# Transposes of the attention output and of the decayed keys: from TensorE to DMA, in a two-layer hybrid decoder step

## The chip, the cores and the metric

One Trainium2 chip, all 8 of its cores. Each core runs the same program on its own share: one prompt sequence of 2048 tokens (with 16 meta tokens ahead of it) and 16 of the 128 sample sequences of 4 tokens each. The cores don't talk to each other. The metric is the device time in microseconds of the slowest core.

## The reference

Two layers, each with two branches on the same normalised input, and gates that merge them:

```python
xn = rmsnorm(h, norm_g)
q, k, v, ga, u, gb, alow, mg = split(xn @ w_in)
la = log_sigmoid(alow @ w_alpha + b_alpha) / 16          # per token and key channel
# branch A, gated linear attention: 4 heads, keys 128 wide, values 256 wide
b = cumsum(la)                                           # within a chunk
o = (q exp(b)) (k exp(-b))^T, causal, @ v  +  (q exp(b)) @ S
S = exp(b_C) * S + (k exp(b_C - b))^T @ v                # b_C: b of the chunk's last token
o = o * rsqrt(mean(o*o) + EPS) * gla_gain * silu(ga)
ya = o @ w_a
# branch B: trailing means over 2/4/8/16 tokens minus the token, a small product, silu(gb), @ w_b
merged = sigmoid(mg_a + bias) * ya + sigmoid(mg_b + bias) * yb
h = h + merged @ w_out
```

Returned are the final outputs of prompt and samples and the new states of both branches. What the change touches is `o` after its norm, and `k exp(b_C - b)`, the decayed keys that go into the state S.

## The kernel before

**Tiling.** Activations lie transposed in on-chip memory (features on the 128 partitions, tokens along the row): XN is the normalised input, OT the finished output of branch A, YP that of branch B, MB decays and later the merged result. Tokens are cut into five chunks c = 0 to 4 of 464, 384, 384, 384 and 512 columns; chunk 0 holds the samples (64 columns), the 16 meta tokens and three prompt tiles of 128 tokens, the others 3, 3, 3 and 4 prompt tiles. Matrix products are bf16 with f32 sums.

**Stages.** Per layer: norm and transpose of the input (`stage_d`), decays (`alpha`), branch B (`pool_unit`), then attention as 4 heads times 5 chunks of `att_unit`, then for each of 8 column blocks and 5 chunks a `merge_unit`, which reads all heads' blocks of OT. Head 0 is woven with branch B, and heads 1 to 3 run with `sample_batch` (per head four of them, each with a load of 512 KB of sample states and a store of as much) and `sample_out` between the units.

**An attention unit** (`att_unit`, L902): keys are projected and scaled; GpSimd multiplies them by the decay at the tile's end into kdT (features on partitions); queries and values are projected (v_tok: tokens on partitions, two buffers that units take in turn); scores are computed and masked into ATm. kdT is needed with tokens on partitions. TensorE transposes it, one instruction for each 128x128 block, into a PSUM bank, and ScalarE copies the bank to kd_tok. Then two projections of the gate path go through tanh into the buffers zb. Then tiles are taken in pairs (one pair and one single tile where a chunk has three): `kd_tok x v` gives the state's increment (`bp`), two products give the output `o_`, VectorE updates the state (f32) and casts it to bf16 for the next tile, ScalarE squares and sums `o_`, GpSimd does the inverse root, and ScalarE writes the normalised output `on`. At the unit's end TensorE transposes `on`, two blocks for each tile, into a bank, and VectorE multiplies it with gain and gate into OT.

**What sets the order.** `Sched` records all operations; `list_schedule` then fixes one order for each engine beforehand, by assumed costs and by the order of recording. On the chip every engine, TensorE and the SyncE queue (SP) too, works in that fixed order and waits where an operand is not there. For its plan a DMA on SP is assumed to cost the queue 60 ns, to occupy a transfer resource shared by all DMAs for bytes / 200 ns, and to land 1.8 us later. Waits come from keys: a region of X or Y has one key for each 256 bytes of a row.

**Lines.** Products are recorded at L551, transposes at L556, scalar_tensor_tensor at L591, copies and casts at L598, tensor_tensor at L579, DMAs at L611; they are helpers, so a group of the trace is told by its tiles. All of kdT, kd_tok, on, ATm, v_tok, the states and zb lie in sb_X; sample states, their bf16 copy and kdm in sb_Y. `sb_ident_bf,sb_X` at L556 is thus a transpose of kdT or on, `sb_Y<-sb_ar,sb_invcnt` the build of kdm, the masked sample keys (kd0 in sb_ar times the masks in sb_invcnt).

Of the kernel before, what the change touches and what calls it, by code (L numbers as in the profile page):

```python
# [7 lines left out]
F32 = mybir.dt.float32  # L8
# [5 lines left out]
NL = 2  # L14
# [353 lines left out]
def build_nc():  # L368
# [30 lines left out]
    with contextlib.ExitStack() as st:  # L399
# [25 lines left out]
        X = Region("X", 25600)  # L425
# [10 lines left out]
        negc = sb("negc", [128, NCOLS], F32)  # L436
# [22 lines left out]
        kd_tok, kd_tok_k = X.take(512, BF16)  # L459
        ATm, ATm_k = X.take(512, BF16)  # L460
        on, on_k = X.take(1024, BF16)
        zb = [X.take(512) for _ in range(3)]
# [42 lines left out]

        def ot_rest(c):
            return ["ot%d_%d" % (c, h) for h in range(1, 4)] + (["ots_%d" % h for h in range(1, 4)] if c == 0 else [])


        mrg = []  # L510
        for i in range(2):
            a = X.take(512, at=2048 + i * 4096)
            b = X.take(512, at=2048 + i * 4096 + 2048)
            mrg.append((a, b))
        a = X.take(512, at=0)
        b = X.take(512, at=10240)
        mrg.append((a, b))
# [164 lines left out]
        def consts():  # L682
# [3 lines left out]
            ts("dve", negc[:, :], cols[:, :], -1.0, r=["cols"], w=["negc"])  # L686
# [95 lines left out]
        def alpha(l, c, wal):  # L782
# [9 lines left out]
            for h in range(4):  # L792
                bl, blk = bank("G")
                mm(bl[:, 0:N], wst[:, h * 128:(h + 1) * 128], ast[:, 0:N], True, True, r=["wst", "ast"],
                   w=[blk])
                act(b_ap(c, h), bl[:, 0:N], AF.Exp, r=[blk, "negc"], w=b_keys(c, h),
                    bias=negc[:, l * 40 + CL_BA + h:l * 40 + CL_BA + h + 1], scale=-1.0)
# [104 lines left out]
        def att_unit(l, h, c, wqk, wv, wga):  # L902
# [9 lines left out]
            v_ap, vk = v_tok[p]  # L912
            ek, bk = "ebc%d" % p, b_keys(c, h)
# [64 lines left out]
            bt, btk = bank("G")  # L978
            btb = bfv(bt)
            for j in range(nt):  # L980
                s_ = slice(base + j * 128, base + (j + 1) * 128)
                tr(btb[:, j * 128:(j + 1) * 128], kdT[:, s_], ident_bf[:, :], r=kdT_k + ["ident_bf"], w=[btk])
            if c == 0:
                tr(btb[0:NM, 512:640], kdT[:, 0:NM], ident_bf[:, :], r=kdT_k + ["ident_bf"], w=[btk])
                cp("act", kd0[0:NM, :], btb[0:NM, 512:640], r=[btk], w=kd0_k)
            cp("act", kd_tok[:, 0:nt * 128], btb[:, 0:nt * 128], r=[btk], w=kd_tok_k)
# [25 lines left out]
            for j0 in range(0, nt, 2):  # L1012
# [9 lines left out]
                for jj, j in enumerate(pr):  # L1022
# [325 lines left out]
```

How the kernel before makes its waits and increments, by code:

```python
            def run_engine(ename, eng):  # L294
                seen = {}
                for op in ops:
                    if op["eng"] != ename:
                        continue
                    need = {}
                    for d in op["kept"]:
                        sk, val = ops[d]["token"]
                        if need.get(sk, 0) < val:
                            need[sk] = val
                    items = [(sk, val) for sk, val in need.items() if seen.get(sk, 0) < val]
                    attach = items.pop() if (items and op.get("attach")) else None
                    for sk, val in items:
                        eng.wait_ge(sems[sk], val)
                        seen[sk] = val
                    inst = op["fn"](eng)
                    if attach is not None:
                        inst._wait_ge(sems[attach[0]], attach[1])
                        seen[attach[0]] = attach[1]
                    if op["token"] is not None:
                        sk, val = op["token"]
                        inst.then_inc(sems[sk], 16 if op["dma"] else 1)
                if ename == "sp":
                    for k, v in self.dma_final.items():
                        sk = ("dma",) + k
                        if seen.get(sk, 0) < v:
                            eng.wait_ge(sems[sk], v)
```

## Time and profile before

| | us |
|---|---|
| time, median of 3 runs (lowest to highest) | 1240.41 (1240.02 to 1241.66) |
| the profiled execution: its time | 1240.96 |
| its span on the slowest core (core 6) | 1239.1 |
| spans of the eight cores | 1231.7 to 1239.1 |
| granted clock, mean of each core | 0.982 to 0.988 |
| VectorE, ScalarE, GpSimd busy | 709.3, 554.7, 463.7 |
| queue of hardware DMAs (SP): MB, share of 16 engines' span | 81.46, 20.2% |
| queue of software DMAs (GpSimd): MB, share | 35.98, 18.8% |

A busy time adds up instructions from start to end; those of TensorE overlap a little, as their ends are modelled. "Idle before, releaser" is the time in which an engine stood before instructions of a group, and what ended it. A DMA's landing is the time from issue to completion.

### The profile page before, as it was taken

How to read it: one execution, taken by the hardware profiler on the slowest of the kernel's cores; microseconds unless marked ns; L12 is line 12 of the kernel's file. 1: busy time of each engine (PE TensorE's matmuls, PEld its weight loads, DVE VectorE, ACT ScalarE, POOL GpSimd, SP SyncE). 2: the span in 40 equal slices, each digit the busy share in tenths (PEclk: the TensorE clock that was granted, in tenths of full speed). 3: DMA queues.
4: the chain of work that ended last, by engine and by line, in shares of the span. 5: the costliest groups of instructions: out<-in, count | busy, mean ns of one | idle time of the engine just before them, and what ended most of it. 6: DMA issues, size and time to landing. Idle time of an engine off the chain costs nothing.

```text
span 1239.1 us, 22649 instructions; the slowest of 8 cores (1231.7 to 1239.1 us)
## 1 busy us (share of the span) xinstructions
PE 1159.9 (94%) x7554; PEld 694.3 (56%) x7616; DVE 709.3 (57%) x1278; ACT 554.7 (45%) x1255; POOL 463.7 (37%) x730
## 2 busy tenths in 40 slices
PE   2778889999999999999999899999999999999997
PEld 1434446677676555555545555676767655555543
DVE  6478867767675222237676876676777422223555
ACT  3555455665664222222653644656656422222222
POOL 3268655333333222221236666433342222222221
PEclk9789899999999999999999999999999999999999
DMA  9711037252429113114364513725242813211544
GB/s 238 150 52 39 18 67 174 77 137 77 112 69 189 31 30 64 19 29 154 133 165 135 103 38 84 145 66 131 69 103 86 190 30 58 37 18 26 179 160 156
DMA packets 68591, 118.90 MB, mean 96 GB/s; under 512 B 4188, under 2 KB 46556, under 8 KB 68442
## 3 DMA queue, kind: packets, MB, share of 16 engines
q1 hardware_dynamic: 48570, 81.46, 20.2%
q0 software_dynamic: 19904, 35.98, 18.8%
q8 instruction: 60, 0.98, 0.3%
q14 instruction: 57, 0.47, 0.1%
HBM read 117.89 MB, written 36.24 MB: 124 GB/s over the span
## 4 chain that ended last, share of the span: by engine, by line
PE 82%; DVE 7%; issue 4%; ACT 3%; POOL 2%; DMA 2%; SPq 0%; DVEq 0%; POOLq 0%; ACTq 0%
PE bank L551 79%; PE bank L556 3%; DVE sb_X L598 1%; DVE sb_OT L591 1%; DVE sb_MB L804 1%; DMA sb_Y<-xp 1%; DMA sb_RG<-wpk 1%; DVE sb_Y L585 1%; POOL sb_OT L579 1%; ACT sb_Y L570 1%; DVE sb_XN L579 1%; ACT sb_MB L570 1%; DVE sb_X L591 1%; DVE sb_Y L591 1%; ACT sb_OT L570 1%
## 5 line engine op out<-in xcount | busy, mean ns | idle before, releaser
L551 PE MATMUL bank<-sb_XN,sb_RG 128*128 128x384 bf16 (+2 forms) x3244 | 662.8, 348 | 15.7 <-DVE sb_OT L591 4.8
L551 PEld LDWEIGHTS bank<-sb_XN,sb_RG 128*128 128x128 bf16 x3280 | 318.5, 99 | 256.5 <-issue 18.1
L591 DVE SCALAR_TENSOR_TENSOR sb_X<-sb_X,bank 128x384 f32<-128x384 f32 (+2 forms) x240 | 141.1, 595 | 266.2 <-PE bank L551 238.1
L570 ACT ACTIVATE sb_X<-bank,sb_halfc 128x384 f32<-128x384 f32 (+2 forms) x160 | 98.1, 614 | 257.6 <-PE bank L551 222.5
L570 ACT ACTIVATE sb_X<-bank 128x256 bf16<-128x256 f32 (+6 forms) x328 | 146.3, 463 | 107.9 <-PE bank L551 94.4
L579 POOL TENSOR_TENSOR sb_MB<-sb_X 128x384 bf16<-128x384 f32 (+2 forms) x80 | 88.6, 1108 | 193.4 <-DVE sb_X L591 193.0
L551 PE MATMUL bank<-sb_RG,sb_XN 128*128 128x256 bf16 (+1 forms) x1088 | 146.5, 274 | 2.5 <-DVE sb_OT L591 2.5
L551 PE MATMUL bank<-sb_OT,sb_RG 128*128 128x384 bf16 (+2 forms) x677 | 142.5, 344 | 3.6 <-DVE sb_OT L591 3.4
L570 ACT ACTIVATE sb_Y<-sb_Y 128x1024 bf16<-128x1024 f32 (+1 forms) x79 | 83.3, 1055 | 116.8 <-DVE sb_Y L591 106.2
L579 POOL TENSOR_TENSOR sb_OT<-sb_OT 128x398 f32<-128x398 f32 (+12 forms) x122 | 109.2, 895 | 35.4 <-ACT sb_OT L570 16.8
L551 PE MATMUL bank<-sb_RG,sb_MB 128*128 128x512 bf16 (+1 forms) x523 | 121.5, 379 | 1.0
L551 PEld LDWEIGHTS bank<-sb_RG,sb_XN 128*128 128x128 bf16 (+1 forms) x1088 | 104.9, 99 | 18.9 <-issue 2.9
L551 PEld LDWEIGHTS bank<-sb_OT,sb_RG 128*128 128x128 bf16 x680 | 66.5, 98 | 61.5 <-DVE sb_OT L591 7.0
L551 PE MATMUL bank<-sb_X 128*128 128x256 bf16 (+2 forms) x520 | 86.1, 260 | 8.8 <-DVE sb_X L598 8.3
L551 PEld LDWEIGHTS bank<-sb_RG,sb_MB 128*128 128x128 bf16 (+1 forms) x544 | 53.4, 99 | 58.1
L579 POOL TENSOR_TENSOR sb_X<-sb_X,sb_ebc 128x384 bf16<-128x384 bf16 (+1 forms) x40 | 35.3, 882 | 125.6 <-DVE sb_X L598 88.6
L611 POOL DMA_DIRECT2D sb_RG<-wpk x60 | 46.4, 773 | 86.3 <-PE bank L551 77.7
L570 ACT ACTIVATE sb_OT<-bank 128x384 f32<-128x384 f32 (+7 forms) x120 | 48.4, 438 | 66.6 <-PE bank L551 24.1
L591 DVE SCALAR_TENSOR_TENSOR sb_OT<-bank,sb_halfc,sb_X 128x384 bf16<-128x384 bf16 (+1 forms) x80 | 47.9, 639 | 46.9 <-PE bank L556 46.7
L587 POOL TENSOR_SCALAR sb_rst<-sb_rst 128x1 f32<-128x1 f32 (+1 forms) x51 | 13.2, 258 | 161.8 <-ACT sb_Y L570 154.9
L591 DVE SCALAR_TENSOR_TENSOR sb_X<-sb_X,sb_ebc,bank 128x256 f32<-128x256 f32 x128 | 60.8, 475 | 19.3 <-PE bank L551 18.9
L551 PE MATMUL bank<-sb_YP,sb_RG 128*128 128x384 bf16 (+2 forms) x319 | 70.4, 343 | 0.1
(93 smaller groups left out, 1211.6 us busy)
## 6 DMA issues: line engine op xcount, KB each, us to landing
sb_RG<-wpk POOLq DMA_DIRECT2D x40, 512.0 KB, 7.4
sb_Y<-sgla SPq DMA_DIRECT2D x32, 512.0 KB, 3.9
nsg_s<-sb_Y SPq DMA_DIRECT2D x32, 512.0 KB, 3.0
sb_Y<-xp SPq DMA_DIRECT2D x28, 512.0 KB, 4.7
sb_RG<-wpk POOLq DMA_DIRECT2D x16, 896.0 KB, 10.6
H<-sb_Y SPq DMA_DIRECT2D x16, 512.0 KB, 3.7
sb_Y<-H SPq DMA_DIRECT2D x16, 512.0 KB, 3.7
y_p<-sb_Y SPq DMA_DIRECT2D x16, 512.0 KB, 2.6
```

Of the source, the lines that this page charges most:

```text
L551: return S.add("pe", lambda e: e.matmul(out, lhsT=lhsT, rhs=rhs, start=start, stop=stop, skip_group_check=sgc), r=r, w=w, cost=c, lat=300. ...
L556: return S.add("pe", lambda e: e.transpose(out, in_, ident), r=r, w=w, cost=c, lat=300.0, attach=True)
L570: return S.add("act", lambda e: e.activation(out=out, in_=in_, func=func, **kw), r=r, w=w, cost=c, lat=150.0, tset=tset)
L579: return S.add(eng, lambda e: e.tensor_tensor(out=out, in0=in0, in1=in1, op=op), r=r, w=w, cost=cost or ecost(eng, fsz(out)), lat=150.0)
L585: return S.add(eng, lambda e: e.tensor_scalar(out=out, in0=in0, scalar1=s1, scalar2=None, op0=op0), r=r, w=w, cost=c, lat=150.0)
L587: return S.add(eng, lambda e: e.tensor_scalar(out=out, in0=in0, scalar1=s1, scalar2=s2, op0=op0, op1=op1), r=r, w=w, cost=c, lat=150.0)
L591: return S.add("dve", lambda e: e.scalar_tensor_tensor(out=out, in0=in0, scalar=scalar, in1=in1, op0=op0, op1=op1), r=r, w=w, cost=ecost(" ...
L598: return S.add(eng, lambda e: e.tensor_copy(out=out, in_=in_), r=r, w=w, cost=ecost(eng, fsz(out), 0.7 if eng == "dve" else 1.0), lat=150.0)
L611: return S.add(eng, lambda e: e.dma_start(out=out, in_=in_, **kw), r=r, w=w, dma=True, after=after, cost=nb / 200.0)
L804: S.add("dve", lambda e, h=h: e.tensor_tensor_scan(out=b_ap(c, h), data0=rm[:, 0:N], data1=b_ap(c, h), initial=0.0, op0=ALU.mult, op1=ALU. ...
```

## The change

kdT and `on` are no longer transposed on TensorE. For kdT one DMA with `transpose=True` on the SP queue writes kd_tok for all tiles of a unit; bank, transposes and ScalarE's copy go, except for the 80 columns of samples and meta tokens in chunk 0, which stay on TensorE. For `on` each pair of tiles has two DMAs, one for each half of the head's 256 columns, straight into OT, and VectorE multiplies OT in place. To make room for transfers in flight there are two kd_tok and four zb, `on` is written over the values v_tok of its own tiles, and the buffers of `merge_unit` are laid out anew, its first one in Y. The negated bias shrinks to what is used. kdm is built in four pieces of 512 columns, one in each `sample_batch`, and no longer in one piece of 2048 in the first. In the diff, repeated bookkeeping is cut.

```diff
-        X = Region("X", 25600)
+        X = Region("X", 26624)
...
-        kd_tok, kd_tok_k = X.take(512, BF16)
+        kd_toks = [X.take(512, BF16) for _ in range(2)]
         ATm, ATm_k = X.take(512, BF16)
-        on, on_k = X.take(1024, BF16)
-        zb = [X.take(512) for _ in range(3)]
+        zb = [X.take(512) for _ in range(4)]
...
+        mrg = [(X.take(512, at=i * 4096), X.take(512, at=i * 4096 + 2048)) for i in range(3)]
+        mrg_first = (Y.take(512, at=14848), Y.take(512, at=16896))
...
-            bt, btk = bank("G")
-            btb = bfv(bt)
-            for j in range(nt):
-                s_ = slice(base + j * 128, base + (j + 1) * 128)
-                tr(btb[:, j * 128:(j + 1) * 128], kdT[:, s_], ident_bf[:, :], r=kdT_k + ["ident_bf"], w=[btk])
+            dma(V(kd_tok, nt, 128), kdT[:, base:N], r=kdT_k, w=kd_tok_k, transpose=True)
             if c == 0:
+                bt, btk = bank("G")
+                btb = bfv(bt)
                 tr(btb[0:NM, 512:640], kdT[:, 0:NM], ident_bf[:, :], r=kdT_k + ["ident_bf"], w=[btk])
                 cp("act", kd0[0:NM, :], btb[0:NM, 512:640], r=[btk], w=kd0_k)
-            cp("act", kd_tok[:, 0:nt * 128], btb[:, 0:nt * 128], r=[btk], w=kd_tok_k)
...
-                    o_list.append((o_, bok, on[:, j * 256:(j + 1) * 256], on_k[2 * j:2 * j + 2]))
+                    on = v_ap[:, j0 * 256:(j0 + len(pr)) * 256]
+                    o_list.append((V(o_, 2, 128), bok, V(on, 2, len(pr) * 128)[:, :, jj * 128:(jj + 1) * 128], vkk))
                 gi = (2 * u + j0 // 2) % 4
                 att_norm(o_list, 128, "gs%d" % gi, 4 * gi)
+                m = len(pr)
+                for d in range(2):
+                    blk = ot_blk(c, 2 * h + d)[:, base + j0 * 128:base + (j0 + m) * 128]
+                    gc = l * 40 + CL_GAIN + 2 * h + d
+                    ok = "ot%d_%d_%d%d" % (c, h, d, j0 // 2)
+                    dma(V(blk, m, 128), v_ap[:, (j0 * 2 + d * m) * 128:(j0 * 2 + (d + 1) * m) * 128], r=vkk, w=[ok],
+                        transpose=True)
+                    stt(blk, blk, halfc[:, gc:gc + 1], zs[d][0][:, base + j0 * 128:base + (j0 + m) * 128], ALU.mult,
+                        ALU.mult, r=[ok, "halfc"] + zs[d][1], w=[ok])
                 yield
-            bT, bTk = bank("G")
-            bTb = bfv(bT)
-            for d in range(2):
-                for j in range(nt):
-                    tr(bTb[:, (d * nt + j) * 128:(d * nt + j + 1) * 128],
-                       on[:, j * 256 + d * 128:j * 256 + (d + 1) * 128], ident_bf[:, :],
-                       r=on_k[2 * j:2 * j + 2] + ["ident_bf"], w=[bTk])
-            for d in range(2):
-                gc = l * 40 + CL_GAIN + 2 * h + d
-                stt(ot_blk(c, 2 * h + d)[:, base:N], bTb[:, d * nt * 128:(d + 1) * nt * 128], halfc[:, gc:gc + 1],
-                    zs[d][0][:, base:N], ALU.mult, ALU.mult, r=[bTk, "halfc"] + zs[d][1], w=["ot%d_%d" % (c, h)])
...
-            if j == 0:
-                tt("pool", V(kdm[0:NM, :], NSS, 128), kd0[0:NM, :].unsqueeze(1).to_broadcast([NM, NSS, 128]),
-                   rowm[0:NM, 0:16].unsqueeze(2).to_broadcast([NM, NSS, 128]), ALU.mult, r=kd0_k + ["inv"], w=kdm_k)
+            km = kdm[0:NM, 512 * j:512 * j + 512]
+            kmk = kdm_k[4 * j:4 * j + 4]
+            tt("pool", V(km, 4, 128), kd0[0:NM, :].unsqueeze(1).to_broadcast([NM, 4, 128]),
+               rowm[0:NM, 4 * j:4 * j + 4].unsqueeze(2).to_broadcast([NM, 4, 128]), ALU.mult, r=kd0_k + ["inv"], w=kmk)
...
+            if cb == 0 and c == 1:
+                (a_ap, ak), (b_ap_, bk) = mrg_first
+                cnt["mrg"] = 0
+            else:
+                (a_ap, ak), (b_ap_, bk) = mrg[cnt["mrg"] % 3]
+                cnt["mrg"] += 1
```

## Rows read from the trace of the kernel before

**Rows 1.** Page, part 1: busy us of each engine, share of the span, instructions.

```profile
PE 1159.9 (94%) x7554; PEld 694.3 (56%) x7616; DVE 709.3 (57%) x1278; ACT 554.7 (45%) x1255; POOL 463.7 (37%) x730
```

**Rows 2.** Page, part 2: 40 slices of 31 us: PE busy, granted clock, in tenths.

```profile
PE   2778889999999999999999899999999999999997
...
PEclk9789899999999999999999999999999999999999
```

**Rows 3.** Stretches: bounds, length; busy PE, PEld, DVE, ACT, POOL; clock, DMA share, GB/s.

```profile
228.00:285.00 57.00, 53.88 (x443) 37.74 (x443) 42.07 (x93) 34.90 (x97) 22.65 (x37) 1.00 0.41 103
285.00:342.00 57.00, 55.99 (x463) 40.10 (x465) 39.46 (x92) 35.31 (x97) 19.04 (x35) 1.00 0.37 94
342.00:400.00 58.00, 57.39 (x459) 39.97 (x463) 37.72 (x90) 33.25 (x89) 17.72 (x33) 1.00 0.57 128
```

**Rows 4.** Groups of instructions, shapes apart: the transposes that go.

```profile
L556 PE MATMUL bank<-sb_ident_bf,sb_X 128*128 128x128 bf16 x384 | 41.2, 219 | 0.2
```

**Rows 5.** Timeline of TensorE in one unit: start us, length us, what.

```profile
358.45 0.39 PE L556 MATMUL bank<-sb_ident_bf,sb_X 128*128 128x128 bf16 x4
358.67 0.38 PE L551 MATMUL bank<-sb_ar,sb_Y 80*128 80x256 bf16 x2
...
360.03 0.66 PE L551 MATMUL bank<-sb_X 128*128 128x256 bf16 x6
```

**Rows 6.** Timeline of GpSimd, same unit: decayed keys written.

```profile
353.25 0.83 POOL L579 TENSOR_TENSOR sb_X<-sb_X,sb_ebc 128x384 bf16<-128x384 bf16 x1 [6.08 <-DVE sb_X L598]
```

**Rows 7.** Groups, shapes apart: other engines' work that the change touches.

```profile
L579 POOL TENSOR_TENSOR sb_Y<-sb_ar,sb_invcnt 80x2048 bf16<-80x2048 bf16 x8 | 29.5, 3687 | 0.0
...
L591 DVE SCALAR_TENSOR_TENSOR sb_OT<-bank,sb_halfc,sb_X 128x384 bf16<-128x384 bf16 x64 | 36.6, 613 | 45.3 <-PE bank L556 45.1
...
L570 ACT ACTIVATE sb_X<-bank 128x384 bf16<-128x384 bf16 x32 | 15.6, 486 | 0.9 <-PE bank L556 0.9
...
L591 DVE SCALAR_TENSOR_TENSOR sb_OT<-bank,sb_halfc,sb_X 128x512 bf16<-128x512 bf16 x16 | 11.2, 745 | 1.6 <-PE bank L556 1.6
```

**Rows 8.** Waits of TensorE: waited for, us in total, times, longest.

```profile
PE bank L551 <- DVE sb_X L598: 8.3, 9, 1.7
```

**Rows 9.** Timeline, all engines, around the start of head 2's first unit.

```profile
281.27 3.60 POOL L579 TENSOR_TENSOR sb_Y<-sb_ar,sb_invcnt 80x2048 bf16<-80x2048 bf16 x1
...
283.09 1.94 DVE L598 CAST sb_X<-sb_X 128x256 bf16<-128x256 f32 x1
...
285.09 0.39 PE L551 MATMUL bank<-sb_X 128*128 128x256 bf16 x2 [1.15 <-DVE sb_X L598]
```

**Rows 10.** Transfers of the whole run: count, KB each, median us to landing.

```profile
sb_Y<-sgla SPq DMA_DIRECT2D x32, 512.0 KB, 3.9
nsg_s<-sb_Y SPq DMA_DIRECT2D x32, 512.0 KB, 3.0
...
nsg_p<-sb_X SPq DMA_DIRECT2D x8, 128.0 KB, 4.4
...
nsp_s<-sb_OT SPq DMA_DIRECT2D x8, 32.0 KB, 1.7
```

**Rows 11.** Timeline in head 1: GpSimd writes decayed keys, SyncE issues a load.

```profile
251.20 0.82 POOL L579 TENSOR_TENSOR sb_X<-sb_X,sb_ebc 128x384 bf16<-128x384 bf16 x1 [6.63 <-DVE sb_Y L598]
...
251.61 0.38 SPq L611 DMA_DIRECT2D sb_Y<-sgla  x1
```

**Rows 12.** Transfers between 372 and 405 us, end of layer 0's attention.

```profile
nsg_s<-sb_Y SPq DMA_DIRECT2D x1, 512.0 KB, 14.8
...
nsg_p<-sb_X SPq DMA_DIRECT2D x1, 128.0 KB, 12.2
```

**Rows 13.** Timeline, last unit of layer 0: GpSimd, SyncE, TensorE in turn.

```profile
374.04 1.04 POOL L579 TENSOR_TENSOR sb_X<-sb_X,sb_ebc 128x512 bf16<-128x512 bf16 x1 [6.78 <-DVE sb_X L598]
...
374.15 5.96 SPq L611 DMA_DIRECT2D sb_Y<-xp  x2
...
384.11 0.71 PE L551 MATMUL bank<-sb_X 128*128 128x256 bf16 x5
```

More of the change, by code:

```diff
@@ L435, in build_nc @@
         cols = sb("cols", [128, NCOLS], F32)
-        negc = sb("negc", [128, NCOLS], F32)
+        negc = sb("negc", [128, 4 * NL], F32)
         halfc = sb("halfc", [128, NCOLS], F32)
@@ L504, in build_nc, with ot_keys @@
         utok, utok_k = ob(4, 512, "utok")
+        def ot_keys(c, hs):
+            ks = ["ot%d_%d_%d%d" % (c, h, d, j) for h in hs for d in range(2) for j in range(2)]
+            return ks + (["ots_%d" % h for h in hs] if c == 0 else [])
         def ot_rest(c):
[L507 to L517, printed above, removed]
+            return ot_keys(c, range(1, 4))
+        mrg = [(X.take(512, at=i * 4096), X.take(512, at=i * 4096 + 2048)) for i in range(3)]
+        mrg_first = (Y.take(512, at=14848), Y.take(512, at=16896))
         Y.pos = 0
@@ L685, in consts @@
             cp("dve", invcnt[:, :], cft[:, CF_INVCNT:CF_INVCNT + 84], r=cft_k, w=["inv"])
-            ts("dve", negc[:, :], cols[:, :], -1.0, r=["cols"], w=["negc"])
+            for l_ in range(NL):
+                ts("dve", negc[:, 4 * l_:4 * l_ + 4], cols[:, l_ * 40 + CL_BA:l_ * 40 + CL_BA + 4], -1.0, r=["cols"],
+                   w=["negc"])
             cp("pool", ident_f[:, :], cft[:, CF_IDENT:CF_IDENT + 128], r=cft_k, w=["ident_f"])
@@ L796, in alpha @@
                 act(b_ap(c, h), bl[:, 0:N], AF.Exp, r=[blk, "negc"], w=b_keys(c, h),
-                    bias=negc[:, l * 40 + CL_BA + h:l * 40 + CL_BA + h + 1], scale=-1.0)
+                    bias=negc[:, 4 * l + h:4 * l + h + 1], scale=-1.0)
             yield
@@ L912, in att_unit @@
             v_ap, vk = v_tok[p]
+            kd_tok, kd_tok_k = kd_toks[p]
             ek, bk = "ebc%d" % p, b_keys(c, h)
@@ L1001, in att_unit @@
                 proj(bg[:, 0:N], wga[0], wga[1], c, bgk, w0=d * 1024)
-                z_ap, zk = zb[cnt["z"] % 3]
+                z_ap, zk = zb[cnt["z"] % 4]
                 cnt["z"] += 1
@@ L1079, in sample_batch @@
                     mm(bp[:, jj * 256:(jj + 1) * 256], kdm[0:NM, s * 128:(s + 1) * 128], v0[0:NM, :], True, True,
-                       r=kdm_k + v0_k, w=[bpk])
+                       r=kmk + v0_k, w=[bpk])
                 for jj in range(2):
@@ L1110, in merge_unit @@
             N = C_LEN[c]
-            (a_ap, ak), (b_ap_, bk) = mrg[cnt["mrg"] % 3]
-            cnt["mrg"] += 1
+            if cb == 0 and c == 1:
[4 more added lines that the diff above has]
+                cnt["mrg"] += 1
             w_ap, wk = wc
@@ L1121, in merge_unit @@
             yield
-            okeys = ["ot%d_%d" % (c, h) for h in range(4)] + (["ots_%d" % h for h in range(4)] if c == 0 else [])
+            okeys = ot_keys(c, range(4))
             bya, byak = bank("G")
@@ L1250, in build_nc @@
                 S.alias(ot_rest(c), ob_keys[c])
-            dma(nsp_s[l, :, 0:11, :], spool[l, :, 4:15, :], r=["ot0_0"], w=[])
+            dma(nsp_s[l, :, 0:11, :], spool[l, :, 4:15, :], r=["ot0_0_00"], w=[])
             for h in range(1, 4):
```

## The prediction

> **What bounds the kernel now.** I read the page's totals first: TensorE is busy for 1159.9 us, 94% of the span [rows 1]. The slices say where the rest lies: TensorE is under nine tenths in the first six of 40, in one in the middle and in the last, and at nine or more elsewhere, nearly always at the full granted clock [rows 2]. Busy matmuls prove little by themselves, so I took the busy time of single heads, cut where one head's first chunk follows the last of the head before. Heads 1 to 3 of layer 0 take 57, 57 and 58 us, with TensorE busy for 53.9, 56.0 and 57.4 of these, VectorE for 38 to 42, ScalarE for 33 to 35, GpSimd for 18 to 23 [rows 3]. So in the stage that the change touches TensorE sets the pace, and each step taken out of its queue comes off the time, if nothing else becomes late.
>
> **What goes from TensorE.** The code gives the count: a head has 16 prompt tiles, each with one block of kdT and two of `on`; 48 blocks, 4 heads, 2 layers: 384, and the trace has the same 384 at 41.2 us [rows 4]. That busy time is not the price, as a matmul's record lasts past the start of the next. The price is the step from start to start: four transposes begin at 358.45 and the next product at 358.67, so 0.22 us / 4 = 55 ns [rows 5]. 384 x 55 ns = 21.1 us. The products around them stay. All of it lies on the path while TensorE is the bound: **-21.1 us**.
>
> The Trainium skill speaks against this edit. "VectorE: DVE Perf Modes", section "The three transpose paths", prices a 128x128 bf16 transpose at 390 ns on TensorE and 1309 ns by DMA, and advises TensorE wherever PSUM is a fit destination. The 390 ns don't agree with this trace: 384 of them would be 150 us, and the trace's step is 55 ns. The 1309 ns no row here shows; what they would do is a rival below.
>
> **The new wait for the decayed keys.** 40 DMAs (one for each unit) take the place of transposes and a ScalarE copy. Who waits: the `bp` product, and behind it on TensorE everything, as its order is fixed. In the unit shown kdT is written at 353.25 + 0.83 = 354.08 [rows 6], and the first products on sb_X that can read kd_tok start at 360.03 [rows 5]: 5.95 us. With nine transposes (0.5 us) gone from between, the cover is about 5.5 us. The trace has no transposing DMA. The nearest rows are plain ones on the same queue: 32 KB lands in 1.7 us, 512 KB in 3.0 to 3.9, 128 KB from sb_X in 4.4 [rows 10]. A kdT of three tiles has 96 KB. All these ends lie under 5.5 us, so I take 0 for the ordinary unit. For the upper end, suppose that it queues behind a state load: rival 1.
>
> **At the end of the attention.** There the queues are full: between 372 and 405 us a 512 KB store lands in 14.8 us and a 128 KB one in 12.2 [rows 12]. The last unit's kdT is written at 374.04 + 1.04 = 375.08, two loads are on SP from 374.15 and hold it for 5.96 us, and the first products that need kd_tok start about 384.11 [rows 13]. The cover is 9.0 us, and the landing may be 12 to 15: a stall of 0 to 5.8 us. The last DMAs of `on` may also keep the merge waiting, for no more than about as much. In both layers: 0 to 17 us, price taken **+4 us**, near the low end, since the fixed order puts the merge's projections, already begun there, beside it.
>
> **The normalised output.** 160 DMAs: two halves, two groups, 40 units. Their reader is VectorE, and behind that `merge_unit`, which comes after all heads; inside a head nobody on TensorE waits for them. They hold v_tok and zb, each needed again only two units (20 us) later, against landings of 3 to 4 us [rows 10]: 0. On the SP queue they and the 40 others stand among a head's nine plain DMAs (four loads, four stores, the final state) of 0.38 us [rows 11]. VectorE had 2 operations per unit and gets 4: from 613 ns for 384 columns and 745 for 512 [rows 7], 132 ns for each 128 columns, so 481 for 256 and 349 for 128. A unit of three tiles goes from 2 x 613 = 1226 to 2 x (481 + 349) = 1660 ns, one of four from 1490 to 1924: +0.43 us, 17.4 in all, 2.2 per head, beside 15 to 20 us in which VectorE is idle in a head [rows 3]. These also stand ahead of state updates in its order, and wait on a DMA. Between 0 and the full 17.4 I take **+1.5 us**, near 0 for the idle share. ScalarE loses 40 copies of about 0.49 us [rows 7], which were off the path: 0.
>
> **kdm in four pieces.** A small edit, with a term of its own. GpSimd's one instruction takes 3.69 us, eight times [rows 7]. In head 2 it begins at 281.27 and ends at 284.87; VectorE's cast of the state begins at 283.09 and lasts 1.94 us, to 285.03; and TensorE's products on the state start at 285.09, after 1.15 us of idle time ended by that cast [rows 9]. The cast ends as GpSimd's instruction ends, so I read the one as held by the other. All TensorE waits for that cast come to 8.3 us, nine times [rows 8], and I take eight of them as one for each head. A quarter of 3.69 us and its fixed cost is about 1.0 us, so a cast can be held by 1.0 at most where it was held by up to 3.6. The gain lies between 0 and 8.3; I take **-5 us**, as most of 3.69 goes. Other edits (buffers, bias) issue nothing on the path: 0.
>
> **The sum** against the profiled execution's 1240.96 us: -21.1 - 5 + 4 + 1.5 = -20.6, so 1220.4. That execution is 0.55 us over the median 1240.41: 1219.8, stated as **1220 us**. Its own range goes from 1211 (all of 8.3 gained, no new wait) to 1236.
>
> **Rival 1: the decayed keys queue behind a state load.** Slower. Place: four units of each head have a `sample_batch` whose 512 KB load goes out just ahead of kdT; in the sample at 251.61, while kdT of that unit is written at 251.20 + 0.82 = 252.02 [rows 11]. The load lands in 3.9 us; if the transposing DMA only then takes its own 3.0 us [rows 10], it is there after 6.9, and 1.4 us too late. 32 such units: +45, so about 1265. It decides from a landing of 5.5 us, at 40 us for each us past it. For it: the load goes out on the same queue 0.4 us ahead, and is five times as large. Against it: DMA engines are busy for only 0.37 to 0.57 of a head [rows 3].
>
> **Rival 2: the stream of transposes itself becomes the bound.** Slower. If one queue takes time b for each 128x128 block, a head needs 48 b + 9 x 0.38 us. TensorE would need about 57 - 2.7 = 54.3 us, so b decides at 1.06 us. Rows bound b only from far off: a 512 KB transfer in 3.0 us gives 0.19 us for 32 KB, and a lone 32 KB lands in 1.7 us [rows 10]. I hold it nearer the first, since blocks of one DMA need not wait for each other. At b = 1.2 a head takes 61.0, 4.0 over 57; in the six heads that are not woven with branch B that is +24: 1265, and 29 us more for each further 0.1 us. By the 1309 ns of the Trainium skill ("VectorE: DVE Perf Modes", the same section) a head would take 66.3 us, and the time would be 1297; no run so far shows whether it does. "Advanced Engine Details and Errata" of the Trainium skill, section "X-Bar Transpose (TRN2)", says the contrary, that such DMAs are as fast as others (350 to 400 GB/s), about 0.09 us a block by estimate.
>
> **Rival 3: the gain is eaten by the other engines' chains.** No change. Each unit has a chain from state update to cast to product; with TensorE 5% quicker it comes due sooner, VectorE has 2.2 us more per head, and TensorE waits where it now works: 1238 to 1242. Against it: VectorE is busy for 42 of 57 us at most [rows 3], and its waits on this path are 8.3 us now [rows 8].
>
> That the change doesn't do what it says is no rival of weight: the transposes are plainly taken out.
>
> **How the numbers follow.** Forecast 0.60, rival 1 0.15, rival 2 0.14, rival 3 0.11. Low 1211 is the forecast's best case; below it I leave 0.05. The high end takes in rival 1 and the beginning of rival 2, 1266; beyond it 0.14. 0.2% (2.5 us) is about what a measurement of this kernel can tell from no change: faster holds the forecast and a few weak forms of rival 1, 0.62; same is most of rival 3, 0.10; slower 0.28.
>
> **What would show it.** After: no group of 384 transposes; a group of 200 transposing DMAs with its landing, under 5.5 us if I'm right, and 40 of them with no TensorE wait behind; heads of about 54 us; kdm's 32 pieces near 1.0 us and TensorE's wait for the cast well under 8.3 us. Wrong would be: TensorE's wait before products on sb_X ended by a DMA, over 1 us in most units (rival 1), SP always issuing, and heads over 60 us (rival 2).

## The result and the profile after

The changed kernel takes 1288.34 us (median of four runs) against 1240.47 for the kernel before, a ratio of 1.037 with a 95% interval of 1.034 to 1.040. One of the four, 1437.91 us, was a slow run with a lower clock on one die; the other three took 1283.68 to 1289.06 us, and the ratio is that of such fast runs alone. It is slower by 48 us, where 20 us of gain were forecast, and outside the range of 1211 to 1266. Its profiled execution has a span of 1282.1 us on core 1.

The page after, parts 1 and 2 (busy us; 40 slices of 32 us in tenths), against [rows 1, 2]:

```profile
PE 1157.4 (90%) x7232; PEld 674.0 (53%) x7232; DVE 709.6 (55%) x1359; ACT 535.8 (42%) x1215; POOL 472.9 (37%) x754
PE   2778888889989999999999899977978999999997
PEclk9989989999999999999999999998989999999999
```

TensorE lost 384 transposes, and its busy time fell by 2.5 us only: it has idle time in both attention stretches (of slices 6 to 11, counted from 0, four are at eight tenths, of slices 26 to 30 four at seven or eight), and the granted clock dips in slices 27 and 29. To see where the time went I cut both traces at events that both have: from the first sample product of an attention stretch to the last (products on sb_zq). The view is that of busy time by stretch, columns as in [rows 3]; first the kernel before, then the one after:

```profile
179.00:375.00 196.00, 190.78 (x1587) 135.80 (x1594) 139.66 (x317) 121.73 (x333) 77.33 (x131) 1.00 0.42 106
727.00:960.00 233.00, 228.21 (x1812) 157.15 (x1822) 160.82 (x355) 136.88 (x373) 96.24 (x163) 1.00 0.39 96
```

```profile
182.00:400.00 218.00, 191.03 (x1435) 127.34 (x1434) 141.95 (x351) 113.98 (x318) 79.35 (x140) 0.98 0.55 120
747.00:1006.00 259.00, 228.56 (x1651) 150.62 (x1649) 162.26 (x392) 128.61 (x353) 98.68 (x168) 0.95 0.50 109
```

The stretches grow from 196 to 218 and from 233 to 259 us, together by 48 us. The profiled spans differ by 43.0 us (1239.1 and 1282.1), so all of the loss is here, and outside them 5 us are gained. TensorE's idle time in them grows from 5 + 5 to 27 + 30 us, though it has less to do. Its waits (waited for, us, times, longest), against [rows 8], and under them one wait of VectorE and one of ScalarE from the view of all waits:

```profile
PE bank L548 <- DVE sb_X L595: 28.9, 15, 9.4
PE bank L548 <- DVE sb_X L588: 13.1, 10, 3.0
PE bank L548 <- DMA sb_X<-sb_X: 1.6, 2, 1.3
...
DVE sb_OT L588 <- DMA sb_OT<-sb_X: 71.1, 55, 7.5
...
ACT sb_Y L567 <- DMA sb_Y<-sgla: 40.0, 13, 9.3
```

The decayed keys hardly hold TensorE: it waits 1.6 us for their DMAs in the whole run. It waits 28.9 us for the cast of the state (8.3 before), and VectorE waits 71.1 us, 55 times, at multiplies in OT for transposing DMAs. ScalarE waits 40.0 us for the loads of sample states, where it waited 2.0 us before. What the transposing DMAs cost shows in two views: transfers of the run (count, median us to landing), and the time for which one holds the SP queue (ns, least, median, most):

```profile
sb_OT<-sb_X SPq DMA_TRANSPOSE x160, 3.0
sb_X<-sb_X SPq DMA_TRANSPOSE x40, 2.7
...
sb_Y<-sgla SPq DMA_DIRECT2D x32, 512.0 KB, 4.6
nsg_s<-sb_Y SPq DMA_DIRECT2D x32, 512.0 KB, 4.6
```

```profile
L608 SPq DMA_TRANSPOSE sb_OT<-sb_X x160: 1088/1167/3891, 148.9 to 1026.1; - x160
L608 SPq DMA_TRANSPOSE sb_X<-sb_X x40: 1162/1188/2537, 114.9 to 1002.3; - x40
L608 SPq DMA_DIRECT2D sb_Y<-sgla x32: 379/458/518, 103.3 to 994.6; - x32
```

A transposing DMA holds SP for 1.17 us, three times a plain one, and 20 times what the planner assumed (60 ns). The plain ones behind it land later than in [rows 10]: stores in 4.6 us, not 3.0. Both the landing and the issuing are on the chain of work that ended last (page, part 4, by engine; before, then after):

```profile
PE 82%; DVE 7%; issue 4%; ACT 3%; POOL 2%; DMA 2%; SPq 0%; DVEq 0%; POOLq 0%; ACTq 0%
PE 66%; DMA 9%; DVE 8%; SPq 5%; issue 5%; ACT 4%; POOL 2%; DVEq 0%; ACTq 0%; POOLq 0%
```

Followed back from the ends of the two stretches, the chain has 19.5% and 8.2% of them in landings of the output's DMAs and 14.1% and 12.0% (31 us each) in SP's issuing; before, neither is on it.

How one stall comes about shows in the timeline after, at the end of head 1 (SyncE, GpSimd, VectorE, TensorE in turn; start, length, in brackets the idle time before and what ended it):

```profile
273.57 5.68 SPq L608 DMA_TRANSPOSE sb_OT<-sb_X  x4
...
278.00 0.82 POOL L608 DMA_DIRECT2D sb_RG<-wpk  x1 [0.78 <-PE bank L548]
...
281.13 1.70 DVE L588 SCALAR_TENSOR_TENSOR sb_OT<-sb_OT,sb_halfc,sb_X 128x256 bf16<-128x256 bf16 x3
287.37 0.35 DVE L588 SCALAR_TENSOR_TENSOR sb_OT<-sb_OT,sb_halfc,sb_X 128x128 bf16<-128x128 bf16 x1 [4.54 <-DMA sb_OT<-sb_X]
287.63 0.47 DVE L588 SCALAR_TENSOR_TENSOR sb_X<-sb_X,sb_ebc,bank 128x256 f32<-128x256 f32 x1
...
288.58 0.28 DVE L595 CAST sb_X<-sb_X 128x256 bf16<-128x256 f32 x1
...
288.92 0.39 PE L548 MATMUL bank<-sb_X 128*128 128x256 bf16 x1 [4.44 <-DVE sb_X L595]
```

Four transposes of the output go out one after another from 273.57, the last in the moment in which a weight load starts on GpSimd's queue (278.00). VectorE has done three multiplies and stands at the fourth for 4.54 us. Nobody needs that multiply soon; but in VectorE's fixed order it is ahead of the state update and the cast, and TensorE stands at the product on the state for 4.44 us. The landing depends on what else is under way. Transfers after, first 245 to 267 us, then 268 to 289, where the next head's weights come in:

```profile
nsg_s<-sb_Y SPq DMA_DIRECT2D x3, 512.0 KB, 5.7
sb_Y<-sgla SPq DMA_DIRECT2D x2, 512.0 KB, 5.1
sb_OT<-sb_X SPq DMA_TRANSPOSE x9, 2.9
sb_X<-sb_X SPq DMA_TRANSPOSE x2, 3.1
```

```profile
sb_RG<-wpk POOLq DMA_DIRECT2D x1, 896.0 KB, 11.3
...
nsg_s<-sb_Y SPq DMA_DIRECT2D x1, 512.0 KB, 10.9
sb_OT<-sb_X SPq DMA_TRANSPOSE x4, 4.5
sb_X<-sb_X SPq DMA_TRANSPOSE x2, 7.6
```

Beside weight loads a store lands in 10.9 us instead of 5.7, and keys in 7.6 instead of 3.1.

### The profile page after: what moved, and what is told of

It is laid out like the page before. It is cut to its first block, busy times and chain, and to the rows that moved or that the text cites. A ratio compares the mean times of both kernels' runs of the same rounds, so it can differ in the third digit from the quotient of the medians.

```text
span 1282.1 us, 22819 instructions; the slowest of 8 cores (1261.6 to 1282.1 us)
## 1 busy us (share of the span) xinstructions
PE 1157.4 (90%) x7232; PEld 674.0 (53%) x7232; DVE 709.6 (55%) x1359; ACT 535.8 (42%) x1215; POOL 472.9 (37%) x754
## 4 chain that ended last, share of the span: by engine, by line
PE 66%; DMA 9%; DVE 8%; SPq 5%; issue 5%; ACT 4%; POOL 2%; DVEq 0%; ACTq 0%; POOLq 0%
PE bank L548 65%; SPq L608 5%; DMA sb_OT<-sb_X 5%; ACT sb_X L567 2%; DVE sb_OT L588 2%; DMA sb_Y<-sgla 2%; PE bank L553 1%; DMA sb_X<-sb_X 1%; DMA sb_X<-xp 1%; DVE sb_MB L803 1%; DVE sb_X L588 1%; ACT sb_Y L567 1%; DVE sb_Y L582 1%; ACT sb_OT L567 1%; DVE sb_XN L576 1%
## 5 line engine op out<-in xcount | busy, mean ns | idle before, releaser
L548 PE MATMUL bank<-sb_XN,sb_RG 128*128 128x384 bf16 (+2 forms) x3280 | 675.9, 350 | 18.9 <-DVE sb_OT L588 6.5
L548 PEld LDWEIGHTS bank<-sb_XN,sb_RG 128*128 128x128 bf16 x3280 | 320.8, 99 | 269.4 <-issue 24.3
L567 ACT ACTIVATE sb_X<-bank,sb_halfc 128x384 f32<-128x384 f32 (+2 forms) x156 | 95.3, 616 | 254.0 <-PE bank L548 214.8
L567 ACT ACTIVATE sb_X<-bank 128x256 bf16<-128x256 f32 (+4 forms) x288 | 127.7, 457 | 139.3 <-PE bank L548 120.3
L548 PE MATMUL bank<-sb_RG,sb_XN 128*128 128x256 bf16 (+1 forms) x1088 | 143.9, 278 | 3.5 <-DVE sb_OT L588 2.2
L548 PE MATMUL bank<-sb_X 128*128 128x256 bf16 (+2 forms) x520 | 93.0, 267 | 43.3 <-DVE sb_X L595 28.9
L548 PE MATMUL bank<-sb_RG,sb_MB 128*128 128x512 bf16 (+1 forms) x544 | 125.4, 379 | 0.0
L548 PEld LDWEIGHTS bank<-sb_RG,sb_XN 128*128 128x128 bf16 (+1 forms) x1088 | 108.4, 101 | 24.0 <-issue 3.1
L588 DVE SCALAR_TENSOR_TENSOR sb_OT<-sb_OT,sb_halfc,sb_X 128x256 bf16<-128x256 bf16 (+1 forms) x160 | 71.6, 476 | 71.6 <-DMA sb_OT<-sb_X 71.1
L548 PEld LDWEIGHTS bank<-sb_X 128*128 128x128 bf16 (+1 forms) x520 | 48.2, 100 | 74.8 <-DVE sb_X L595 35.8
L584 POOL TENSOR_SCALAR sb_gst<-sb_gst 128x2 f32<-128x2 f32 (+2 forms) x88 | 19.4, 221 | 146.3 <-ACT sb_X L567 121.7
```

Source lines behind the costliest of these rows:

```text
L548: return S.add("pe", lambda e: e.matmul(out, lhsT=lhsT, rhs=rhs, start=start, stop=stop, skip_group_check=sgc), r=r, w=w, cost=c, lat=300. ...
L567: return S.add("act", lambda e: e.activation(out=out, in_=in_, func=func, **kw), r=r, w=w, cost=c, lat=150.0, tset=tset)
L584: return S.add(eng, lambda e: e.tensor_scalar(out=out, in0=in0, scalar1=s1, scalar2=s2, op0=op0, op1=op1), r=r, w=w, cost=c, lat=150.0)
L588: return S.add("dve", lambda e: e.scalar_tensor_tensor(out=out, in0=in0, scalar=scalar, in1=in1, op0=op0, op1=op1), r=r, w=w, cost=ecost(" ...
```

## Experiments

Theory A: VectorE stands in its fixed order at multiplies whose data land late. Theory B: the decayed keys are late (the prediction's rival 1). Theory C: the DMAs harm by their load on queue and engines, whoever waits. Times are medians; the ratio to the kernel before on the same chip stands behind where a few us matter. The kernel before took 1240 to 1242 us in all sets but one, which is named.

**Which of the two.** Keys by DMA, output on TensorE:

```diff
             dma(V(kd_tok, nt, 128), kdT[:, base:N], r=kdT_k, w=kd_tok_k, transpose=True)
...
-                    dma(V(blk, m, 128), v_ap[...], r=vkk, w=[ok], transpose=True)
-                    stt(blk, blk, halfc[...], zs[d][0][...], ...)
+                    tr(bTb[:, ...], on[:, ...], ident_bf[:, :], r=on_k[...] + ["ident_bf"], w=[bTk])
+                stt(ot_blk(c, 2 * h + d)[:, base:N], bTb[:, ...], halfc[...], zs[d][0][:, base:N], ...)
```

> The changed kernel with the normalised output transposed on TensorE again (bank, multiply once per unit and half, own buffer for the normalised output), the decayed keys still by DMA, kdm still in four pieces. Theory A (the loss comes from VectorE standing in its fixed order at multiplies whose output transposes land late): the loss is gone; 128 blocks off TensorE give 7 us, kdm some us more, so 1228 to 1238 us. Theory B (the decayed keys arrive late, the rival 1 of the prediction): the loss stays here, 1260 us or more. Theory C (any transposing DMA costs by its load on queue and engines, in proportion to their number): a fifth of them is left, so about 1240 to 1250.

Measured: 1219.29 us, ratio 0.982 (0.981 to 0.984), faster than the kernel before and 9 us under the range that A gave. Its attention stretches, and its keys' landing:

```profile
174.00:364.00 190.00, 188.52 (x1531) 132.89 (x1529) 133.64 (x316) 113.33 (x313) 77.82 (x140) 1.00 0.53 119
715.00:941.00 226.00, 225.14 (x1763) 155.37 (x1760) 156.76 (x355) 128.30 (x348) 98.48 (x172) 1.00 0.46 107
```

```profile
sb_X<-sb_X SPq DMA_TRANSPOSE x40, 2.3
```

TensorE is idle for 1.5 and 0.9 us of 190 and 226. The counterpart, output by DMA and keys on TensorE (edit: the keys' `dma` line undone):

> The changed kernel with the decayed keys transposed on TensorE again and copied by ScalarE; the normalised output still by 160 DMAs. Theory A: the loss stays, 1270 to 1295 us. Theory B: it goes, and 256 blocks off TensorE show, 1225 to 1235. Theory C: four fifths of the DMAs are left, 1275 to 1285, and the first kernel of this set tells A from C.

Measured: 1273.31 us (1.026), VectorE's wait for the output's DMAs 57.6 us. B falls; the loss is that of the 160 DMAs. One fifth of the DMAs gives no loss at all, so C in proportion falls too. But the two halves don't add up. Over kdm alone (1227.20 us, below) the output by DMA costs 46 us with the keys on TensorE, and over keys alone it costs 69; keys by DMA gain 8 us by themselves and cost 15 beside the output's. ScalarE's wait for the state loads goes with that: 6.7 us with keys alone, 2.3 with the output alone, 40.0 with both. That it makes the difference was not tested.

**kdm alone**, in the kernel before:

```diff
-            if j == 0:
-                tt("pool", V(kdm[0:NM, :], NSS, 128), ..., w=kdm_k)
+            km = kdm[0:NM, 512 * j:512 * j + 512]
+            kmk = kdm_k[4 * j:4 * j + 4]
+            tt("pool", V(km, 4, 128), ..., w=kmk)
```

> The kernel before with one edit: kdm built in four pieces of 512 columns, one in each sample batch. If the 3.69 us instruction of GpSimd holds VectorE's cast, and that TensorE, up to 8.3 us come back, 5 taken: about 1235 us, with TensorE's wait for the cast under 3 us. If the cast is late for another reason: 1240, the wait unchanged.

Measured: 1227.20 us, ratio 0.988 (0.987 to 0.990): 13 us, not 5. The wait falls nearly as expected (under 3 us), from 8.3 to 3.2:

```profile
PE bank L551 <- DVE sb_X L598: 3.2, 10, 0.5
```

The other 8 us are not in that wait. Is it the order, which the planner makes anew?

> The kernel before, same instructions, with the planner told 1120 ns for the one kdm instruction in place of 3730, so that only the fixed order around it shifts. It measures what a new order alone brings: if the 13 us of the run with kdm in four pieces were mostly a lucky order, 1228 to 1236; if they come from the pieces, 1237 to 1245.

Measured: 1239.87 us (1.000). This new order brings nothing. The stretches outside heads 1 to 3 tell more: first the kernel before, then kdm in four pieces, between the same events (clock, DMA share and GB/s stand last):

```profile
110.00:179.00 69.00, 59.83 (x359) 33.85 (x363) 54.36 (x76) 35.54 (x68) 44.12 (x61) 0.93 0.18 34
681.00:727.00 46.00, 39.54 (x231) 22.98 (x231) 36.85 (x53) 25.64 (x42) 28.11 (x44) 0.93 0.38 70
```

```profile
110.00:174.00 64.00, 56.87 (x360) 32.58 (x361) 53.20 (x77) 36.35 (x69) 44.37 (x65) 0.97 0.19 36
673.00:715.00 42.00, 37.71 (x232) 22.19 (x231) 34.38 (x53) 26.09 (x44) 27.99 (x47) 0.96 0.43 76
```

5 and 4 us go in branch B's stretches, where the clock is granted at 0.97 and 0.96 instead of 0.93 and TensorE idles 2 us less in each. The traces show where. Head 0 builds its kdm within branch B. In layer 0, before, then in four pieces:

```profile
129.43 7.01 DVE L804 TENSOR_TENSOR_SCAN sb_MB<-sb_rmp,sb_MB 128x384 f32<-128x384 bf16 x4 [0.69 <-ACT sb_MB L570]
130.54 4.23 POOL L579 TENSOR_TENSOR sb_Y<-sb_ar,sb_invcnt 80x2048 bf16<-80x2048 bf16 x1
...
137.00 1.04 PE L556 MATMUL bank<-sb_ident_bf,sb_Y 128*128 128x128 bf16 x8 [4.41 <-DVE sb_YP L591]
```

```profile
130.51 4.43 DVE L804 TENSOR_TENSOR_SCAN sb_MB<-sb_rmp,sb_MB 128x384 f32<-128x384 bf16 x4 [0.70 <-ACT sb_MB L570]
...
135.50 0.62 PE L556 MATMUL bank<-sb_ident_bf,sb_Y 128*128 128x128 bf16 x8 [1.83 <-DVE sb_YP L591]
```

Beside GpSimd's long instruction VectorE's four scans take 7.01 us instead of 4.43, TensorE stands behind them for 4.41 us instead of 1.83, and its clock is granted at 0.58 from 135 to 140 us and 0.87 from 140 to 150, instead of 1.00 in both. In layer 1 one multiply of VectorE takes 3.93 us and ends at 721.47, GpSimd's instruction at 721.06; TensorE stands for 1.95 us, and its clock from 722 to 727 is 0.66. So the 3.69 us instruction has victims outside the state's cast as well. The traces show this; no run has the pieces in head 0 alone.

**The planner's issue time.** The changed kernel, same instructions, other order (`xp` is set for transposing DMAs; at 1800 it changes the issue time only):

```diff
                 issue = 60.0 if e == "sp" else 900.0
+                land = 1800.0
+                if op["xp"]:
+                    issue, land = 1170.0, op["xp"]
...
-                done_t[idx] = xfer_start + op["cost"] + 1800.0
+                done_t[idx] = xfer_start + op["cost"] + land
```

> The changed kernel; only the planner that fixes the order of every engine now assumes 1170 ns (the measured median) for the time in which a transposing DMA holds the SP queue, in place of 60; same instructions. Theory A in the form that the order is wrong because of that 60: most of the loss goes, 1225 to 1255 us. If the queue or the landing itself is too slow for the work, whatever the order: 1275 or more.

Measured: 1261.46 us (1.016): 27 us back, though the time stays 6 us above the range that A gave. VectorE's wait for the output's DMAs falls from 71.1 to 17.7 us. Two waits of TensorE grow: for keys to 13.5 us (four times, 8.0 at most), for ScalarE's writes into sb_X from 4.3 to 9.6. With the landing told as well (8 us for the output, 4 for the keys, instead of 1.8):

> The changed kernel; the planner assumes 1170 ns on the SP queue for a transposing DMA and, besides, a landing of 8 us (output) or 4 us (decayed keys) after that, in place of 1.8; same instructions. Theory A (VectorE stands in its order at multiplies whose data land late): the multiplies are put later, VectorE's wait for these DMAs falls under 10 us, and the time falls below the 1261 us of the run with the issue time alone, to 1225 to 1250. Theory C (load of the DMAs as such): no better than 1255.

Measured: 1246.09 us (1.006); again 1250.14 (1.007) in a later set:

> The kernel with the planner told issue and landing (earlier 1.006 of the kernel before), once more, so that it and the next one stand on the same chip: the cut of weight loads was timed on another chip than this one. Within 0.5% of its earlier ratio, 1.001 to 1.011.

VectorE's wait for these DMAs is gone from the list, as A says. Together the two wrong constants make 38 to 42 us. But 1246 is still no better than the kernel before, and 27 over the kernel with keys alone, though TensorE has 256 transposes (14 us) less.

**Load without a reader.** To the kernel with keys alone, 160 surplus transposes of the same sizes:

```diff
                 att_norm(o_list, 128, "gs%d" % gi, 4 * gi)
+                for d in range(2):
+                    dma(V(junk[i_][0], m, 128), XN[:, 8 * C_OFF[c]:8 * C_OFF[c] + m * 128], ..., transpose=True)
```

> The kernel with only the decayed keys by DMA and the output transposed on TensorE (1219 us), and 160 additional transposing DMAs issued at the points at which the changed kernel has them, reading the normalised input and writing a scratch that nobody reads; they are surplus work. Theory A (the wait for the data is the harm): nothing waits for them but what stands behind them on SP, so 1219 to 1240. Theory C (holding the queue and loading the engines is the harm): most of the loss comes back, 1260 or more.

Measured: 1245.34 us (1.004), between both theories: 26 of the changed kernel's 69 us over 1219 come though no engine reads the data. They are not load alone: the surplus DMAs write three scratch buffers in turn, and SP waits 24.3 us (twelve times, 8.6 at most) for an earlier one to land before it issues the next, a wait that the changed kernel doesn't have. So 26 may be too much for the load. Where else it is seen is another wait, that of ScalarE for the sample states, whose loads stand behind the transposes on SP (6.7 us with keys alone):

```profile
ACT sb_Y L569 <- DMA sb_Y<-sgla: 38.1, 13, 6.4
```

> The kernel with 160 surplus transposing DMAs that nobody reads (1245 us), with the planner's issue time for transposing DMAs at 1170 ns. If its 26 us over 1219 come from work planned too early behind a held SP queue (state loads, decayed keys), the planner puts that right: 1222 to 1232. If they come from the load on queue and engines themselves: 1240 or more.

Measured: 1238.20 us (0.998). The planner takes 7 us off, and 19 stay. In its profiled execution four cores have spans of 1213 to 1217 us, and TensorE waits for a keys' DMA for 0.8 us at most on them; on the four at 1233 to 1237 one such wait lasts 12.0, 10.0, 13.3 and 10.9 us (cores 1, 2, 5, 7). It is the last one of layer 0's attention: on core 7 that DMA, issued at 369.9 us, lands after 24.0 us, on core 0 after 6.3. In the stretch from 380 to 395 us, which holds most of the wait, the clock is granted at 0.69 to 0.75 on these four and at 1.00 on core 0. The same kernel is thus at either pace by whether one keys' DMA lands late, and where none does, 160 surplus DMAs cost nothing that can be seen against the spans of 1212.9 to 1218.8 us with keys alone.

**Weight loads.** Those of heads 1 to 3 and the first merge blocks cut to 64 columns, order unchanged (the rest of these weights is left out):

```diff
-            dma(ap[:, 0:width], wpk[l][:, src:src + width], ...)
+            dw = 64 if small else width
+            dma(ap[:, 0:dw], wpk[l][:, src:src + dw], ...)
+            S.ops[-1]["cost"] *= width / dw
```

> The changed kernel (1288 us) with the weight loads of heads 1 to 3 and of the first three merge blocks cut to 64 columns each, in both layers (one load, of cells not yet written, stays whole); the order of all engines is the same, as the planner is told the full size. The rest of those weights is not loaded, so part of the computation is left out. If transposing DMAs that land in 9 us and more beside these loads make the loss, the long landings go and with them 15 to 35 us: 1255 to 1273. If the loss comes from the queue and the order alone: above 1280.

> The same cut of weight loads in the kernel before, as the base for the run above; the same part of the weights is left out. Nothing on its path waits for these loads or for landings beside them, so 1236 to 1241 us.

Measured: 1254.63 us (1.012) for the changed kernel, 34 less; 1240.28 (1.000) for the kernel before. The same loads cost the one nothing and the other 34 us. With them cut, its transposes land in 2.4 us in the median instead of 3.0, and VectorE's longest wait for them is 2.6 us instead of 7.5:

```profile
DVE sb_OT L588 <- DMA sb_OT<-sb_X: 49.6, 50, 2.6
```

And under the planner with measured times:

> The changed kernel with the planner told 1170 ns of issue and 8 or 4 us of landing (1246 us), and the weight loads of heads 1 to 3 and of the first three merge blocks cut as before; that part of the weights is left out. If the 26 us that separate it from the kernel with only the decayed keys by DMA (1219) and its own 14 us less TensorE work are landings beside weight loads, which no constant in the planner covers: 1205 to 1228. If they are state loads held up behind transposing DMAs on SP: above 1238.

Measured: ratio 0.983 (0.982 to 0.985), but on a chip where the kernel before took 1260.40 us: some of its cores have a granted clock of 0.96 there and spans of 1256 to 1259, the others 1232 to 1239 as elsewhere. The ratio can't be set beside those of other chips; its own time, 1239.48, is 7 us under that of e5. Repeated with its base on one chip:

> The same with the cut weight loads (earlier 0.983 of the kernel before on its chip; part of the weights is left out), beside the run above. If landings beside weight loads are the rest of the loss: 20 to 32 us under the run above. If the earlier gap came from the other chip: under 12 us.

Measured: 1239.61 us beside 1250.14, so 10.5 us, and the claim of 20 to 32 falls. Once the order allows for late landings, the weight loads explain a third of the 31 us (1250.14 - 1219.3) for which this kernel stands over the one with keys alone.

**State loads off SP.** On the chip with 1260 us for the kernel before:

```diff
-            dma(V(s_ap, 4, 256), sgla[...], r=[], w=sk)
+            dma(V(s_ap, 4, 256), sgla[...], r=[], w=sk, eng="pool")
```

> The changed kernel with the planner told 1170 ns of issue and 8 or 4 us of landing (1246 us), and the 32 loads of sample states issued by GpSimd in place of SP. If state loads that stand behind transposing DMAs on SP, and ScalarE standing behind them (17.7 us of waits), are what is left of the loss: 1215 to 1235. If it is the landings beside weight loads: 1242 or more, since the loads now share that queue.

Measured: ratio 1.001 (1.000 to 1.003). ScalarE still waits 15.1 us for these loads (17.7 before the edit). The comparison with e5_plan_land runs across two chips, and e13 and e17 show what that is worth: one kernel, 1239.5 us on both, ratios of 0.983 and 0.999. On the cores whose clock is not lower (0.972 to 0.979) the profiled execution has spans of 1236.0 to 1246.7 us, those of e5_plan_land 1234.2 to 1244.2. So no gain is seen, and the 1215 to 1235 expected if these loads were the rest fail.

**Fewer, larger DMAs.** Two per unit for the output, from a buffer of its own:

```diff
+            for d in range(2):
+                dma(V(blk, nt, 128), on[:, d * nt * 128:(d + 1) * nt * 128], r=on_k, w=oks, transpose=True)
```

> Normalised output in a buffer of its own, laid out so that two DMAs per unit (all tiles of a half) transpose it: 80 in place of 160, of the same bytes, the multiply once per half again; decayed keys by DMA; the planner assumes 1170 ns of issue and 4 us of landing. If the price on the SP queue is per instruction (some 1.17 us whatever the size), the queue is held 94 us less, and with it the waits shrink: 1205 to 1235 us. If it is per block or per byte, the issue of one DMA grows to 1.7 us or more, and the time stays at 1250 or more.

Measured: 1320.28 us (1.064), far off. The queue's price is per instruction, as the first half of the expectation says: DMAs of three and four blocks hold SP as long as those of one and two:

```profile
L614 SPq DMA_TRANSPOSE sb_OT<-sb_X x80: 1162/1176/3164, 150.8 to 1063.9; - x80
```

The time is lost elsewhere: this one buffer is written again by the next unit, and ScalarE waits 28.5 us for its release by DMAs of which single ones, beside weight loads, land in 10 to 13 us. TensorE waits 50.0 us for VectorE's writes into sb_X (13.1 in the changed kernel); that the one buffer makes all of this was not shown. Whether fewer DMAs with two buffers would gain was not tried, as there was no room in on-chip memory.

**The version that beats both.** Keys alone, with the planner told of them:

> The kernel with only the decayed keys by DMA (1219 us), with the planner's 60 ns for their issue set to 1170 ns. Five of them per head leave the queue free most of the time, so both theories say no difference beyond what a new order brings, 1214 to 1223; a gain of more than 5 us would say that these too suffered from the order.

> Only the decayed keys by DMA, with the planner told 1170 ns of issue and 4 us of landing in place of 1.8. Its waits for these DMAs are 2 us at most now, so 1213 to 1220 us; it would be the version that beats both kernels.

Measured: 1218.14 us (0.983, 0.981 to 0.984) and 1219.36 us (0.985, 0.980 to 0.989). With five DMAs per head neither constant matters. The best of these kernels is 22 us faster than the kernel before and 70 us than the changed one.

## Why the prediction was wrong, step by step

**TensorE as the bound, 55 ns a transpose (-21.1):** right where it could be seen. Keys by DMA against kdm alone, 1219.3 against 1227.2, is 7.9 us for 128 transposes and 40 copies; 128 x 55 ns is 7.0. For the 256 of the output no run gave the gain.

**Keys, no wait in the ordinary unit (0):** right. 40 DMAs land in 2.3 to 2.7 us in the median under a cover of 5.5, and TensorE waits 1.6 us (1.9 with keys alone). Rival 1 named the wrong victim: what the shared queue delays are the plain state loads behind transposes.

**End of the attention (+4):** of the right kind; 1.9 us with keys alone, in layer 0, and 10.0 to 13.3 us there on four cores of e11_idle_plan, where one DMA landed after 22.7 to 26.5 us. That is more than the 5.8 given for one such stall and within the 0 to 17 for both layers; the 17 doesn't follow from the terms either (two stalls of 5.8 and as much again for the merge are 23).

**The normalised output (+1.5): this step failed.** It said that inside a head nobody on TensorE waits for these DMAs, and priced only VectorE's 17.4 us of longer work. The reader is nobody's supplier, but its place in VectorE's order is ahead of state update and cast. The step named this and gave it no price. Its size is 1288.3 - 1219.3 = 69 us.

Of these, by runs: 27 for the planned issue time and 11 to 15 for the planned landing (A); 27 to 31 stay with right constants, of which weight loads account for 10.5 and the rest is open. TensorE then waits 16.6 us for ScalarE's writes into sb_X and 8.7 for the state's cast, and its clock is granted at 0.97 in the attention (e16_plan_land_again). Two things stand behind ScalarE there: in one place a state load that lands after 10.0 us, for which it waits 11.4 us and TensorE, behind it, 5.42; and the multiplies themselves, which the planner now puts late: ScalarE waits 35.8 us for them (7.8 in the changed kernel, 18.0 for the multiplies with keys alone).

The step also took v_tok as free for two units; ScalarE waits 9.0 us, seven times, in the changed kernel until the output's DMAs have landed. And VectorE's longer work, priced at up to 17.4 us, was 24.5 us in these multiplies (47.8 to 72.3), while its busy time as a whole stayed at 709 us, in part as the casts of the state took 42.8 us instead of 56.0.

The 160 DMAs without reader cost 26 with waits of SP's own among it; the 19 after replanning are, in the profiled execution, one late landing of keys. ScalarE's waiting for state loads is 38.1 us and 17.5 after replanning; that it makes the loss was not shown, and with the output alone by DMA it is 2.3 us beside a loss of 46. These parts overlap and are not to be added. The 34 us of weight loads in the changed kernel are the same waits seen from the side of the landing.

**Issue time.** I took a head's plain DMAs at 0.38 us and for transposes only asked what would saturate SP, b = 1.06 us a block. The price turned out to be 1.17 us per instruction, whatever its blocks, 29 us of a head's 57 for 25 DMAs. The queue is not full, so rival 2 as priced, a queue that sets the pace of every head, is not it; yet its issuing is 31 us of the chain in each stretch. And I didn't compare that unknown with the planner's 60 ns, on which the whole order hangs.

**kdm (-5):** the wait fell by 5.1 us as reckoned; the time fell by 13. The term took each of GpSimd's eight instructions as holding one cast. In head 0 they held scans and a multiply instead, with TensorE behind them, and 9 of the 13 us go in those stretches.

**The range.** The forecast's own range ends at 1236, with the 17.4 us of VectorE left at nothing; the term's own bound would have put it at about 1254. The measured time is beyond even that, and beyond the 1266 at which the whole range ends.

**The price of a transpose by DMA.** "VectorE: DVE Perf Modes" of the Trainium skill ("The three transpose paths") gives 1309 ns for 128x128 by DMA, and under "Rules for kernel authors" advises TensorE where PSUM will do. That advice holds here for the output (46 to 69 us) and not for the keys, which gain 8 us by DMA. The number is near the 1.17 us for which one instruction holds SP, but that is for up to four blocks. "Advanced Engine Details and Errata" of the Trainium skill ("X-Bar Transpose (TRN2)", as fast as regular DMAs, 350 to 400 GB/s) isn't borne out: before, the hardware queue moved 81.46 MB in 20.2% of 1239.1 us, or 250.3 us of all 16 engines, 325 GB/s; with keys by DMA 4.20 MB more took 35 us more (23.4% of 1218.8 us is 285.2), so 120 GB/s, and with all transposes 12.6 MB took 87 us, 145 GB/s.

## What to carry to other kernels

Price a moved step in the order of the engine that reads it, not only on the engine that it leaves: a late operand that nobody needs stops everything queued behind its reader. Where a planner fixes the order, give it the new instruction's measured issue time and landing before judging the change; here that was 38 to 42 of 69 us. Hold the cover of a moved step against the worst landing beside bulk loads, 14.8 us in the changed kernel and up to 26.5 with surplus DMAs, not against the median of 3. The keys gained under a cover of 5.5 to 9 us because few of theirs land late (13.7 us once in layer 0 with keys alone, 1.9 us of waiting); where one did, it cost four cores about 20 us.

## What the hardware showed that I had not expected

- A transposing DMA holds the SP queue for 1.17 us in the median, with one to four blocks of 128x128 alike; a plain one for 0.33 to 0.60.
- Its landing, 2.3 to 4.0 us in the median by kernel, goes to 7.6 to 9.8 us beside weight loads on the other queue and to 14.8 at the end of the attention, and a plain store's to 10.9.
- The granted clock falls with TensorE's stalls: 0.98 and 0.95 in the attention stretches of the changed kernel, 1.00 in both with keys alone.
- A cast on VectorE ended as GpSimd's 3.6 us instruction ended [rows 9], and so did a multiply of 3.93 us, 0.55 elsewhere; four scans beside it took 7.01 us instead of 4.43. With it in four pieces the mean of the 128 casts went from 438 to 421 ns in the kernel before, and TensorE's wait for them from 8.3 to 3.2 us. "SBUF — State Buffer" of the Trainium skill ("Terms", shared port pair) says that VectorE and GpSimd lock each other out for a full instruction; the rows of the cast, the multiply and the scans agree. The mean of 438 ns beside a median of 294 says that other casts are held too; by what was not traced.
